# Expert lists of 128, 64 and 32 places in a single-core backbone layer, and results stored by token and choice

## What is computed

```python
p_top, g_idx = lax.top_k(softmax(hf @ w_router_group + b_router_group), 1)       # 1 of 4 groups
w_top, e_idx = lax.top_k(softmax(le_sel), 2)                                      # 2 of its 8 experts
w_top = w_top / sum(w_top) * p_top
gates = sum(one_hot(g_idx * 8 + e_idx, 32) * w_top[..., None], axis=-2)
hidden = silu(einsum("bld,edf->blef", h, w_exp_gate)) * einsum("bld,edf->blef", h, w_exp_up)
y = einsum("blef,efd->bld", hidden * gates[..., None], w_exp_down)                # d = 1024, f = 256
x = LN(ALPHA * x + gate2 * y)
```

## Time and profile before

| | |
|---|---|
| reported time, median of 3 runs | 2194.84 us (2194.12 to 2198.97) |
| span of the profiled execution | 2190.1 us |
| what lies around the span, against the median | 4.7 us |
| PE busy | 2001.6 us, 91% |
| DVE busy | 1030.6 us, 47% |
| merge | 1333 to 1725 us |
| route | 1725 to 1866 us |
| experts | 1866 to 2146 us |
| combine | 2148 to 2190 us |

### The profile page before, as it was taken

The page is one execution under the profiler, slowest core; times in us unless marked ns, Lnnn a source line. Parts: engine busy times, 40 slices in busy tenths (PEclk is TensorE's granted clock), DMA queues, the critical chain, the costliest instruction groups (busy, mean ns, idle before and its releaser), DMA issues. The chain is left out here.

```text
span 2190.1 us, 33298 instructions
## 1 busy us (share of the span) xinstructions
PE 2001.6 (91%) x13714; PEld 1170.0 (53%) x13714; DVE 1030.6 (47%) x1998; ACT 493.6 (23%) x1211; POOL 279.8 (13%) x333
## 2 busy tenths in 40 slices
PE   4999999999989999999999979996899994899985
PEld 2554545545456666666666665553455544444432
DVE  4656566565656666666676561000000266222224
ACT  1323314233222333333333331000000000111111
POOL 0030020200210210211101100000000010321202
PEclk8999999999989999999999999998999995899998
DMA  9121201211010110110101014498530444899983
GB/s 320 55 68 48 58 10 49 68 49 39 11 33 12 44 30 16 45 31 16 42 10 39 2 47 145 148 249 207 197 86 12 166 194 192 289 357 420 419 343 149
DMA packets 173670, 258.23 MB, mean 118 GB/s; under 512 B 14695, under 2 KB 142504, under 8 KB 159184
## 3 DMA queue, kind: packets, MB, share of 16 engines
q1 hardware_dynamic: 163608, 235.43, 32.2%
q0 software_dynamic: 8096, 15.75, 2.0%
q10 hardware_dynamic: 1816, 4.93, 0.6%
HBM read 229.55 MB, written 39.10 MB: 123 GB/s over the span
## 5 line engine op out<-in xcount | busy, mean ns | idle before, releaser
L692 PE MATMUL bank<-hT,shared 128*128 128x512 f32 x368 | 179.0, 614 | 0.0
L1532 PE MATMUL bank<-hT,shared 128*128 128x512 f32 x352 | 159.7, 608 | 9.3 <-DVE xT L1908 9.3
L1586 PE MATMUL bank<-kept,hT 128*128 128x512 f32 x320 | 149.6, 604 | 0.0
L2101 DVE SCALAR_TENSOR_TENSOR prod<-gth,bank 128x512 f32<-128x512 f32 x16 | 11.0, 688 | 267.2 <-PE bank L2074 267.2
L1532 PEld LDWEIGHTS bank<-hT,shared 128*128 128x128 f32 x352 | 66.9, 195 | 86.5 <-issue 86.3
L2074 PE MATMUL bank<-yT,wm 128*128 128x512 f32 x256 | 111.2, 592 | 0.0
L1046 ACT COPY DT<-bank 128x512 f32<-128x512 f32 (+1 forms) x120 | 61.8, 515 | 200.5 <-PE bank L799 199.5
L2074 PE MATMUL bank<-hT,wm 128*128 128x512 f32 x224 | 97.9, 595 | 3.1 <-DVE prod L2103 3.1
L1282 DVE TENSOR_TENSOR D_<-D_,bank 128x512 f32<-128x512 f32 x80 | 55.0, 687 | 93.9 <-PE bank L799 93.9
L692 PEld LDWEIGHTS bank<-hT,shared 128*128 128x128 f32 x368 | 63.6, 190 | 54.8 <-issue 50.0
L1586 PEld LDWEIGHTS bank<-kept,hT 128*128 128x128 f32 x320 | 57.5, 189 | 62.6 <-issue 60.4
(11 more groups left out here) (438 smaller groups left out, 3702.6 us busy)
## 6 DMA issues: line engine op xcount, KB each, us to landing
shared<-in_w_in_dram SPq DMA_DIRECT2D x58, 512.0 KB, 5.5
kept<-in_w_ada_dram SPq DMA_DIRECT2D x8, 2048.0 KB, 12.8
yd<-mzero SPq DMA_DIRECT2D x1, 16128.0 KB, 97.5
ring<-in_w_exp_gate_dram SPq DMA_DIRECT2D x12, 1024.0 KB, 13.6
ring<-in_w_exp_up_dram SPq DMA_DIRECT2D x12, 1024.0 KB, 17.7
ring<-in_w_exp_down_dram SPq DMA_DIRECT2D x12, 1024.0 KB, 19.1
kept<-in_w_exp_down_dram SPq DMA_DIRECT2D x10, 1024.0 KB, 16.8
aw<-in_w_ada_dram SPq DMA_DIRECT2D x8, 1024.0 KB, 23.6
```

Source lines behind the costliest of these rows:

```text
L692: last = pe.matmul(bank[LATB[j]][:, :], wof(j)[:, k, :], hT[:, k, SEQ:T], start=(k == 0), stop=(k == KD - 1), skip_group_check=True)
L1532: pe.matmul(bank[a][:, :], wn(n)[:, k, :], hT[:, k, SEQ:T], start=(k == 0), stop=(k == KD - 1))
L1586: last = pe.matmul(bank[Z][:, :], hT[:, k, t * P:(t + 1) * P], wz[:, k, :], start=(k == 0), stop=(k == KD - 1), skip_group_check=True)
```

## The change

1. **Rows of three kinds.** The ranking now puts the fixed experts last. Ranks 0 to 4 get 128 places, 5 to 16 get 64, 17 to 26 get 32, and the fixed ones 64 each. That fills NP = 16 rows: five with one list, eight with two (two of them of fixed experts), two with four, and one with 32, 32 and 64. LISTED gives the order of passes. `first` and `cap` need more DVE steps.
2. **Free buffers by pass.** SLOT_OF, FREED and LOADS are worked out on the host: an expert takes the weight buffer that was freed first.
3. **One index.** h2 is stored twice per token, `h2d` and `yd` have 1280 rows, and `idx` is 2 * token + choice. It serves the gather and the scatter; `dest` is gone.
4. **Plain loads in combine.** The two results of a token lie side by side, so SP loads them with five DMAs of 1 MB in place of POOL's ten gathers.
5. **No zeros.** Every row of `yd` is written, so the 16 MB of zeros in merge are gone. The unused places of `lists` are filled with a number out of bounds.

```diff
-NFIX, NBIG = 5, 12
-NP = NBIG + (NX - NBIG) // 2
-NMORE = (2 * T) // (SLOT + 1)
+QUART = 32
+NFIX, NBIG, NMID = 5, 5, 12
+NSMALL = NX - NFIX - NBIG - NMID
+R_MID, R_SMALL, R_FIX = NBIG, NBIG + NMID, NX - NFIX
+CAP = [P] * NBIG + [SLOT] * NMID + [QUART] * NSMALL + [SLOT] * NFIX
+FIRST = [sum(CAP[:r]) for r in range(NX)]
+NP = sum(CAP) // P
+NMORE = (2 * T + NSMALL * (SLOT - QUART - 1)) // SLOT
+SIDES = [[(r, FIRST[r] - n * P) for r in range(NX) if FIRST[r] // P == n] for n in range(NP)]
+LISTED = [14, 15, 0, 13, 5, 1, 6, 11, 2, 7, 8, 3, 12, 9, 10, 4]
+PASSES = [tuple(r for r, _ in SIDES[n]) for n in LISTED]
...
@@ merge
-                    if n == 1:
-                        sp.wait_ge(zero_ready, 1)
-                        sp.dma_start(yd.rearrange("(p b) (c n) -> p (b c) n", p=SLOT, c=4),
-                                     zero[0:SLOT, :].unsqueeze(1).broadcast_to([SLOT, NPLACE // SLOT * 4, D // 4])).then_inc(yz_out, 16)
...
-                act.wait_ge(yz_out, 16)
...
@@ route
-                    sp.dma_start(h2d[t * P:(t + 1) * P, :], h2[:, t % 2, :]).then_inc(h2_out[t % 2], 16)
+                    sp.dma_start(h2d[2 * t * P:2 * (t + 1) * P, :].rearrange("(p a) n -> p a n", a=2),
+                                 h2[:, t % 2, :].unsqueeze(1).broadcast_to([P, 2, D])).then_inc(h2_out[t % 2], 16)
...
-                st.link(TS(out=cap[:, :], in0=rk[:, :], scalar1=float(NBIG), scalar2=float(SLOT), op0=ALU.is_lt, op1=ALU.mult))
-                st.link(STT(out=first[:, :], in0=rk[:, :], scalar=float(NBIG), in1=rk[:, :], op0=ALU.min, op1=ALU.add))
-                st.link(TS(out=first[:, :], in0=first[:, :], scalar1=float(SLOT), scalar2=None, op0=ALU.mult))
+                st.add(dve.tensor_copy(rks[:, 0, :], rk[:, :]))
+                st.link(TS(out=rks[:, 1, :], in0=rk[:, :], scalar1=1.0, scalar2=None, op0=ALU.add))
...
-                st.link(STT(out=empty, in0=ends[:, 0:NP], scalar=cols[:, S_TOK:S_TOK + 1], in1=empty, op0=ALU.add, op1=ALU.add))
-                st.link(TS(out=dest[:, :], in0=empty, scalar1=-float(P), scalar2=None, op0=ALU.add))
...
@@ experts
+        SLOT_OF, LOADS, FREED, free = {}, {}, {}, [(NB - 1, None)]
+        loads = [0] * NB
+        for n, p in enumerate(PASSES):
+            for at, r in zip(AT[n], p):
+                if r >= R_FIX:
+                    SLOT_OF[at] = r - R_FIX
+                else:
+                    SLOT_OF[at], FREED[at] = free.pop(0)
+                    loads[SLOT_OF[at]] += 1
+                    LOADS[at] = loads[SLOT_OF[at]]
+            free += [(SLOT_OF[at], n) for at in AT[n]]
+        LAST_IN = {SLOT_OF[at]: PASS_OF[at] for at in sorted(SLOT_OF)}
...
-            if len(PASSES[p]) == 1:
-                return ((slice(0, P), AT[p][0] % NB),)
-            return tuple((slice(a * SLOT, (a + 1) * SLOT), at % NB) for a, at in enumerate(AT[p]))
+            return tuple((slice(o, o + CAP[r]), SLOT_OF[at]) for at, (r, o) in zip(AT[p], SIDES[LISTED[p]]))
...
-                    if n >= NB:
-                        sp.wait_ge(gu_done, PASS_OF[n - NB] + 1)
+                    if FREED[n] is not None:
+                        sp.wait_ge(gu_done, FREED[n] + 1)
...
-                sp.wait_ge(dn_done, max(PASS_OF[n] for n in range(NX - NB, NX) if n % NB in (2, 3)) + 1)
+                sp.wait_ge(dn_done, max(LAST_IN[2], LAST_IN[3]) + 1)
...
@@ combine
                 for t in range(NT):
+                    sp.dma_start(yg[:, t, :, :], yd[2 * t * P:2 * (t + 1) * P, :].rearrange("(p a) n -> p a n", a=2)).then_inc(got[t], 16)
+                for t in range(NT):
...
-                for t in range(NT):
-                    for n in range(2):
-                        pool.indirect_dma_start(out=yg[:, t, n, :], out_offset=None, in_=yd,
-                                                in_offset=bass.IndirectOffsetOnAxis(ap=slots[:, t, n:n + 1], axis=0)).then_inc(got[t], 16)
```

More of the change, by code:

```diff
@@ L107, in small_constants @@
     tok = np.arange(P)[:, None] + P * np.arange(NT)[None, :]
-    return np.concatenate([np.broadcast_to(row, (P, row.size)), tok, np.broadcast_to(end, (P, end.size)), own,
+    pair = np.concatenate([2 * tok, 2 * tok + 1], 1)
+    return np.concatenate([np.broadcast_to(row, (P, row.size)), pair, np.broadcast_to(end, (P, end.size)), own,
                            np.broadcast_to(last, (P, last.size)), edge, beyond], 1).astype(np.float32)
@@ L222, in build @@
                 wo_in = [sem(f"wo_in{n}") for n in range(2)]
-                stage(merge, bank, yd, hT, oT, yT, mT, shared, cT, ada, w_ada, b_ada, w_in, w_gdn_out, w_ssd_out, kept, wo, wo_in, w_o)
+                stage(merge, bank, hT, oT, yT, mT, shared, cT, ada, w_ada, b_ada, w_in, w_gdn_out, w_ssd_out, kept, wo, wo_in, w_o)
             x1d = nc.dram_tensor("x1d", [T, D], F32, kind="Internal").ap()
@@ L246, in build @@
                 pt = beside[:, :].rearrange("p (t n) -> p t n", n=D)
-                stage(route, bank, C, cols, small, xg, idxs, got, dest, half, mT, ada, pos, x_prompt, x_sample, w_o, ln1_g, ln1_b, w_router_group,
+                stage(route, bank, C, cols, small, xg, idxs, got, half, mT, ada, pos, x_prompt, x_sample, w_o, ln1_g, ln1_b, w_router_group,
                       b_router_group, w_router_expert, b_router_expert, h2d, x1d, lists, yd, idx, slots, wts, more, order, wgu, wdn, wo, wo_in, pt, w_exp_gate, w_exp_up, w_exp_down)
@@ L256, in build @@
                 g2 = sb("g2", [P, 2, D], F32, tail)
-                stage(experts, bank, C, cols, slots, xg, idxs, got, dest, idx, more, order, lists, h2d, yd, w_exp_gate, w_exp_up, w_exp_down, wgu, wdn,
+                stage(experts, bank, C, cols, slots, xg, idxs, got, idx, more, order, lists, h2d, yd, w_exp_gate, w_exp_up, w_exp_down, wgu, wdn,
                       x1, g2, lg2, lb2, x1d, ada, ln2_g, ln2_b)
-                stage(combine, bank, C, ring, half, slots, wts, yd, x1, lg2, lb2, y_prompt, y_sample)
+                stage(combine, bank, C, ring, half, wts, yd, x1, lg2, lb2, y_prompt, y_sample)
 def condition(nc, sb, sem, bank, cst, C, cols, hT, cT, modT, cwT, vecT, half, shared, first_in, x_prompt, x_sample, c,
@@ L2116, in _, with route @@
                     turn(n)
-def route(nc, sb, sem, bank, C, cols, small, xg, idxs, got, dest, half, mT, ada, pos, x_prompt, x_sample, w_o, ln1_g, ln1_b, w_router_group,
+def route(nc, sb, sem, bank, C, cols, small, xg, idxs, got, half, mT, ada, pos, x_prompt, x_sample, w_o, ln1_g, ln1_b, w_router_group,
           b_router_group, w_router_expert, b_router_expert, h2d, x1d, lists, yd, idx, slots, wts, more, order, wgu, wdn, wo, wo_in, pt, w_exp_gate, w_exp_up, w_exp_down):
@@ L2421, in _ @@
                 st.link(dve.tensor_tensor_scan(out=upto[:, :], data0=cst_one, data1=nmore[:, :], initial=0.0, op0=ALU.mult, op1=ALU.add))
-                st.link(TS(out=cap[:, :], in0=cap[:, :], scalar1=float(SLOT), scalar2=None, op0=ALU.add))
                 st.link(TT(out=far[:, :], in0=upto[:, :], in1=nmore[:, :], op=ALU.subtract))
@@ L2425, in _ @@
                 st.link(TT(out=far[:, :], in0=far[:, :], in1=cap[:, :], op=ALU.subtract))
[L2426 removed]
+                st.link(TT(out=far[:, :], in0=far[:, :], in1=first, op=ALU.subtract))
                 places = bank[7][:, 0:NT * NX].rearrange("p (t e) -> p t e", e=NX)
[L2428 to L2430 removed]
+                over_t = lambda one: one.unsqueeze(1).broadcast_to([P, NT, NX])
+                st.link(TT(out=past[:, :, :], in0=places, in1=over_t(cap[:, :]), op=ALU.is_ge))
+                st.link(TT(out=past[:, :, :], in0=past[:, :, :], in1=over_t(far[:, :]), op=ALU.mult))
                 st.link(TT(out=place[:, :, :], in0=places, in1=over_t(first), op=ALU.add))
@@ L2472, in load_expert, with experts @@
         eng.dma_start(to, one.rearrange("(p k) f -> p k f", p=P)).then_inc(signal, 16)
-def experts(nc, sb, sem, bank, C, cols, slots, xg, idxs, got, dest, idx, more, order, lists, h2d, yd, w_exp_gate, w_exp_up, w_exp_down, wgu, wdn,
+def experts(nc, sb, sem, bank, C, cols, slots, xg, idxs, got, idx, more, order, lists, h2d, yd, w_exp_gate, w_exp_up, w_exp_down, wgu, wdn,
             x1, g2, lg2, lb2, x1d, ada, ln2_g, ln2_b):
```

108 lines of the change are left out of this document (50 added, 58 removed).

## The result

The changed kernel takes 2159.45 us (median of four runs, 2156.69 to 2172.37), the kernel before 2194.48 in the same job: a ratio of 0.984, 95% interval 0.981 to 0.988. The profiled execution has a span of 2154.8 us where it was 2190.1, so 35.3 us are gone, not 44.3. The time lies in the predicted range and 9 us above the predicted value. Single executions of one kernel, the one before too, differ by up to 23 us, and in the two long ones that were traced (2206 and 2175 us) some 15 us of it lie ahead of the experts; so I count inside a stage, in each trace.

The account below looks back on a forecast made before the run. PE was taken to pace the first two thirds of the experts and the DMA engines the last third, with a stall from the zeros in merge. Terms -30.9 + 0.6 - 15 + 1 + 0 = -44.3 gave 2150.5 us, range 2138 to 2165.

Parts of the forecast that it names:

- Step 1: Merge: without the 16 MB of zeros PE's whole stall for a slab goes, -30.9 us.
- Step 2: Route: more small DVE operations in the sort, second copy of h2 covered, +0.6 us, bounds 0 to 3.
- Step 3: Experts: six passes fewer, stage becomes bound by transfers at 420 GB/s, -15 us, bounds -27 to 0.
- A: Whole kernel: the main forecast, 2150.5 us, experts 15 us shorter; own range 2142 to 2160, chance 0.73.
- rival C: Experts gain nothing: SP's issue in one order leaves holes that idle the engines; 15 us of holes give 2165; chance 0.09.
- The 12 us of unevenness: End of experts, kernel before: unequally loaded engines put the end at 2127, not a level 2115; 7 us taken for the new kernel.
- rival B: Experts: fuller rows even out the engines and SP's order never starves them, -27 us, 2138; chance 0.09.
- The added time for PE's clock: End of experts: PE waits in passes 12 to 14 and starts each time with the clock down, 4 us added.
- Rival D: Experts, row of 32, 32 and 64: widths don't overlap, gate_up and down come twice, 10.6 us; 2160; chance 0.05.
- Step 4: End of experts: x1's load ends 5 us behind the last store, POOL's drain covers 5.3; +1 us, bounds 0 to 5.
- Step 5: Combine: plain loads stay covered by PE's residual, 0 us; uncovered they would gain or lose some 2.
- The figure of 358 GB/s: Experts, counter-evidence: at this HBM limit of one core 95.4 MB take 266 us, ending at 2139 with no gain.

Follow-up runs that it names:

- the run with both edits: Changed kernel with the mixed row's list of 64 as two halves of 32 and the lists' scatters late: 2153.99 us, ratio 0.982.
- the three last orders: Changed kernel with all edits together, and that with two other orders of rows and SP's loads: 2147.14, 2140.85 and 2142.43 us.
- order p: Changed kernel with all edits, both rows of four lists moved later, SP's loads issued as buffers come free: 2140.85 us, ratio 0.978.

## Why the prediction was right or wrong

**Step 1** held to a tenth of a microsecond, and the zeros put back cost what they had: 31.6 in the trace, 31.4 in the medians. One count in it was short: the two slabs are 4.2 MB, not 2, and would take 20 us at 207 GB/s. They had 44, so nothing hung on it.

**Step 2**: +1.0 for +0.6. On DVE the way from the sort's first operation to `idx` grew from 16.73 us (1843.12 to 1859.85) to 17.31 (1810.06 to 1827.37), the 0.6 of the count. The other 0.4 is in the boundary ahead of the first load. The second copy of h2 stayed covered.

**Step 3** is the failed one: -15 forecast, -6.3 measured, between A and rival C. Its frame was right: transfers bind at 420 GB/s, PE waits ahead of the passes 7 and 12 (16.4 and 17.6 us; said: some 20 and 12), four lists of 32 run side by side at 0.43 us a round (1954.56 to 1954.99 in pass 7).

The term that was mis-sized is lost transfer time. The forecast put the last weights 239 us behind the first load: 227 of bytes and 12 lost, 5 at the start and 7 at the end. They landed at 247.8, so 20.8 were lost, 8.8 more, which is the whole miss of 8.7. The part behind them was right: 18 us to the last store forecast, 18.4 measured.

Where the 20.8 went: 10.6 at the start, of which the scatters' packets are some 5 (with them late, the first three windows lose 5.8 and 4.6); the prediction has no term for them. 4.5 at the first row of four, by rival C's mechanism: SP waits in order for a down buffer behind a long wait of PE. The rest, some 5, lies in the last stretch, where SP stands still in the same way; how it splits between that and unequal engines is not shown.

The 12 us of unevenness in the kernel before were read rightly. Its 227 us of bytes, 10.2 lost at the start and 9.7 at PE's pace end at 2115, the prediction's own level end, and the last weights landed at 2127.0, as it said. Now the engines end level (share 0.98 at 2078, 0.08 at 2082). So rival B's mechanism came too, and its gain was used up by the start and the holes. What the prediction overrated is PE's pace as the bound: it said for two thirds of the stage, and by the windows the engines run at 420 GB/s from 90 us into it (1958), with only 9.7 us lost to that pace.

The added time for PE's clock was there: behind the long wait the first matmuls of the row of four take 1.03 us instead of 0.59 (at 1948.70), at a granted clock of 0.50, which is the lower level of 1.2 GHz, and its gate_up takes 9.4 us (1948.70 to 1958.12). The last stretch grew by 4.9 us, where 4 were added for this; how much of the 4.9 is the clock is not shown.

**Rival D** was given 5%, and its mechanism is simply what happened: 32 and 64 columns don't run side by side. A step over k takes 1.98 us (1871.86 to 1873.84). A step in one width takes 0.86 (two rounds of 0.43), so two steps one after the other would be 1.72: nothing overlaps, and each of the two changes of width costs about 0.13 more. This agrees with the rule cited from the Trainium skill, TensorEngine Tiling (Array Packing), Key Properties. My price of 10.6 was low: gate_up grew by 8.9 and down by 4.4, 13.3 us. And yet taking it away alone moved nothing that could be measured; the run with both edits says why: the scatters had already put the engines behind. I was wrong on the chance and on the size, and the cover was one that I hadn't seen. That the time came out at D's 2160 all the same is chance, since D's mechanism did not make it.

**Step 4**: +4.0 for +1, within its bounds of 0 to 5. I let x1's landing run beside a drain of fixed length. The load itself landed 7 us behind the store, not 5; with a drain of 5.3 that alone would have been some 2. The drain was no fixed cost; it grew from 5.33 to 9.16 us beside the load, since the store that it waits for landed later, and that made it 4.

**Step 5** held: -0.9, and gathers instead of loads change nothing.

**The figure of 358 GB/s** from the Trainium skill (DMA: Bandwidth & Descriptors, Specifications) would have left no gain in the stage. The stage did gain, and windows of the changed kernel show 414 to 424 GB/s. As before the measurement decides.

**The total** is 9.0 us above the forecast: 8.7 in the experts, 3.0 at the barrier and 0.4 in route, less 2.2 ahead of the merge block and 0.9 in combine. The last two no step had; that they took some of the miss back is luck.

Open are the worth of the first hole alone, how the last stretch's loss splits, what the order of the rows is worth without SP's order, and which of the three last orders is best.

## What to carry to other kernels

Before a stage is costed by its bytes, add up from its windows what the engines lose now, stretch by stretch, and say for each stretch what fills it; what replaces a slow engine's pace may be a hole nearly as long. Fixed windows catch what moves into them as well, so take beside them the landing of the last load, counted from the first. An edit that does nothing alone can be one of two costs that cover each other: take the suspects away together before calling either harmless. Where a barrier waits for the drain behind a store, a load that runs beside that store makes it land later and lengthens the drain.

## What the runs showed that I had not expected

- Ten scatters of 128 words of 4 bytes each held the engines at a share of 0.96 with 280 GB/s; with them gone the same stretch moved 424.
- POOL's drain behind an indirect store took 4.9 us with the engines free, 5.3 before, 7.0 in order p and 9.2 to 9.6 beside the x1 load. In the same order the store itself took 3.2, 2.6, 5.3 and some 7.5 us to land.
- Widths of 32 and 64 columns in turn: 1.98 us for a step that takes 0.86 in one width.
